# More slots of the expert loop per unit of work in nine stages of a two-layer kernel

## The reference

```python
def peer(h, w_q, keys, u, v):
    ...
    qh = (x @ w_q).reshape(T, PEER_HEADS, 2, PEER_HALF)
    s = jnp.einsum('thcd,hcnd->thcn', qh, keys).astype(jnp.float32)
    s1, i1 = lax.top_k(s[:, :, 0], PEER_TOPK)
    s2, i2 = lax.top_k(s[:, :, 1], PEER_TOPK)
    ...
    def block(args):
        xb, eb, gb = args
        act = jax.nn.gelu(jnp.einsum('thkd,td->thk', u[eb], xb))
        return jnp.einsum('thk,thkd->td', (gb * act).astype(xb.dtype), v[eb])
```

## Time and profile before

| | |
|---|---|
| time, median of 3 runs | 4246.91 us (4234.9 to 4251.95) |
| time of the profiled execution | 4234.23 us |
| its span, first to last instruction | 4232.1 us |
| busy share of the span | PE 70%, DVE 71%, POOL 38%, ACT 34% |
| DMA | 1521.91 MB, mean 360 GB/s |
| mean granted TensorE clock | 0.852 of 2.4 GHz |

### The profile page before, as it was taken

One profiled execution on the slowest core, in us unless ns is written; L12 is line 12 of the kernel. 1 busy time (PEld: TensorE's weight loads), 2 busy tenths in 40 slices (PEclk: granted clock), 3 DMA queues, 4 the chain that ended last, 5 costly groups with the idle time before them and its releaser, 6 DMA issues.

```text
span 4232.1 us, 32788 instructions
## 1 busy us (share of the span) xinstructions
PE 2981.6 (70%) x9343; PEld 1539.7 (36%) x9343; DVE 3022.8 (71%) x6125; ACT 1425.6 (34%) x4133; POOL 1623.8 (38%) x1311
## 2 busy tenths in 40 slices
PE   4699766876777645757778776868775887555565
PEld 1365352454433202423463233543453633212221
DVE  0406779978988666787669868769786787666666
ACT  1213323522233313246423333523552233322232
POOL 0001332434544434344334434435343345544554
PEclk8798887988989866878889988879887998897888
DMA  8243897989999997999899989999999999999998
GB/s 321 91 162 134 334 405 270 343 343 368 405 367 415 407 413 313 387 387 408 357 359 372 401 361 366 374 365 400 383 371 369 357 416 403 422 421 418 404 421 371
DMA packets 222323, 1521.91 MB, mean 360 GB/s; under 512 B 29758, under 2 KB 33538, under 8 KB 48823
## 3 DMA queue, kind: packets, MB, share of 16 engines
q0 software_dynamic: 187200, 1370.25, 80.6%
q1 hardware_dynamic: 34942, 149.58, 9.0%
HBM read 1516.49 MB, written 3.24 MB: 359 GB/s over the span
## 4 chain that ended last, share of the span: by engine, by line
DMA 31%; PE 30%; DVE 23%; issue 7%; ACT 4%; POOL 3%; DVEq 1%; SPq 1%; PEldq 1%; PEld 0%; ACTq 0%; POOLq 0%
DMA core_ring<-in_l_uv,core_experts 26%; PE sum_rows L1946 8%; DVE core_ring L1906 6%; DVE core_yv L1921 4%; POOL core_ring L1889 3%; PE sum_rows L2213 2%; PE j_in_ps L471 2%; PE j_query_pq L1679 1%; PE s1c_query_pq L1679 1%; PE s1b_in_ps L471 1%; DMA s0a_h_w<-in_l_peer_wq 1%; DMA mod_w<-in_l_w_mod 1%; DMA s1b_h_w<-in_l_peer_wq 1%; PE s0b_out_po L610 1%; DVEq L158 1%
## 5 line engine op out<-in xcount | busy, mean ns | idle before, releaser
L1889 POOL DMA_INDIRECT core_ring<-in_l_uv,core_experts x1280 | 1609.0, 1257 | 2259.7 <-PE sum_rows L1946 1081.4
L1946 PE MATMUL sum_rows<-core_ring,core_diag 128*128 128x512 f32 x3100 | 1681.3, 689 | 670.5 <-ACT core_diag L1935 540.3
L1906 DVE CUSTOM_DVE_ANT_0 core_ring<-core_ring,core_hc 128x1024 f32<-128x1024 f32 x1280 | 1551.8, 1223 | 723.6 <-DMA core_ring<-in_l_uv,core_experts 487.1
L1946 PEld LDWEIGHTS sum_rows<-core_ring,core_diag 128*128 128x128 f32 x3100 | 631.4, 217 | 1643.6 <-ACT core_diag L1935 897.0
L1929 ACT ACTIVATE core_wt<-core_wt 128x1 f32<-128x1 f32 x1280 | 256.5, 200 | 1675.0 <-DVE core_wt L1906 1583.3
L1921 DVE SCALAR_TENSOR_TENSOR core_yv<-core_ring,core_wt,core_yv 128x1024 f32<-128x1024 f32 x495 | 634.0, 1281 | 13.3 <-ACT core_wt L1932 12.8
L1932 ACT ACTIVATE core_wt<-core_wt,core_gates 128x1 f32<-128x1 f32 x1280 | 376.8, 294 | 41.6
L1935 ACT ACTIVATE core_diag<-core_ident,core_wt 128x128 f32<-128x128 f32 x775 | 311.2, 401 | 25.3
L2213 PE MATMUL sum_rows<-core_ring 128*128 128x416 f32 x320 | 118.4, 530 | 5.2 <-DVEq L158 4.1
L1929 ACT ACT_TABLE_LOAD x81 | 103.9, 1283 | 5.2 <-DVEq L158 3.8
L1906 DVE DVE_READ_ACCUMULATOR2_ANT core_wt<- 128x1 f32 x1280 | 104.9, 82 | 0.0
(11 more groups left out here) (772 smaller groups left out, 3055.7 us busy)
## 6 DMA issues: line engine op xcount, KB each, us to landing
mod_w<-in_l_w_mod SPq DMA_DIRECT2D x16, 2048.0 KB, 13.1
core_ring<-in_l_uv,core_experts POOLq DMA_INDIRECT x1280, 10.1
core_ring<-in_l_w_mod POOLq DMA_DIRECT2D x8, 2048.0 KB, 10.9
p_in_w<-in_l_w_in SPq DMA_DIRECT2D x5, 1664.0 KB, 8.9
core_ring<-in_l_w_in POOLq DMA_DIRECT2D x5, 1664.0 KB, 10.6
p_h_w<-in_l_peer_wq SPq DMA_DIRECT2D x16, 512.0 KB, 4.5
s0a_h_w<-in_l_peer_wq SPq DMA_DIRECT2D x16, 512.0 KB, 12.5
s0b_h_w<-in_l_peer_wq SPq DMA_DIRECT2D x16, 512.0 KB, 8.3
```

The lines of the kernel that those rows point to most:

```text
L1889: nc.gpsimd.indirect_dma_start(self.ring[:, r, :], None, core.a[f"l{layer}_uv"], bass.IndirectOffsetOnAxis(ap=self.experts[:, t, n:n + 1], ...
L1906: nc.vector.tensor_tensor_reduce(self.ring[:, r, 0:D], self.ring[:, r, 0:D], self.hc[:], 1.0, 0.0, ALU.mult, ALU.add, self.wt[:, r:r + 1]) ...
L1946: mm = nc.tensor.matmul(self.py[:, c * 512:(c + 1) * 512], self.diag[:, r, :], self.ring[:, r, D + c * 512:D + (c + 1) * 512], start=(at = ...
```

## The change

Nine stages get more slots per unit; leads and places stay.

```diff
-REST_RATES = {"norm": (3.0, PE_4, 5), "gla": (2.0, PE_6, 4), "pool": (2.0, PE_2, 4), "out": (1.5, PE_0, 3), "query": (2.0, PE_0, 2),
+REST_RATES = {"norm": (3.0, PE_4, 5), "gla": (2.0, PE_6, 4), "pool": (2.0, PE_2, 4), "out": (1.75, PE_0, 3), "query": (2.0, PE_0, 2),
...
-LATENT_RATES = {"norm": (3.0, PE_4, 5), "in": (1.0, PE_0, 4), "qk": (1.125, PE_4, 5), "attend": (2.25, PE_5, 3), "out": (1.6, PE_0, 3),
-                "query": (0.9, PE_0, 2), "first select": (2.0, PE_8, 3), "select": (2.1, PE_8, 3)}
+LATENT_RATES = {"norm": (3.0, PE_4, 5), "in": (1.4, PE_0, 4), "qk": (1.125, PE_4, 5), "attend": (2.25, PE_5, 3), "out": (1.9, PE_0, 3),
+                "query": (1.15, PE_0, 2), "first select": (2.0, PE_8, 3), "select": (2.1, PE_8, 3)}
...
-JOINT_RATES = {"norm": (3.0, PE_4, 5), "in": (1.4, PE_0, 4), "qk": (1.125, PE_4, 5), "attend": (2.25, PE_5, 3), "out": (1.6, PE_0, 3),
-               "query": (0.7, PE_0, 2), "first select": (2.0, PE_8, 3), "select": (2.1, PE_8, 3)}
+JOINT_RATES = {"norm": (3.0, PE_4, 5), "in": (1.7, PE_0, 4), "qk": (1.125, PE_4, 5), "attend": (2.25, PE_5, 3), "out": (2.0, PE_0, 3),
+               "query": (1.0, PE_0, 2), "first select": (2.0, PE_8, 3), "select": (2.1, PE_8, 3)}
```

## The result

The changed kernel takes 4191.64 us (median, 4186.9 to 4198.27), the kernel before, run beside it, 4249.43 us (4234.9 to 4260.77). By the medians that is 57.8 us less. The ratio of the runs is 0.9871, with a 95% interval of 0.985 to 0.9893, that is 45.5 to 63.7 us less. Forecast were 4207 us, 40 us less.

A forecast was written before the change was run, and what follows sets the result against it. Gathers bound the drain, while idle DMA time remained in the nine stages; -87.4 + 50.7 - 3 = -40 us took the profiled 4234.2 to 4194 us, or 4207 us against the sister runs' median, range 4172 to 4240.

The forecast's parts named there:

- 768's end: Slot 768's tile end leaves s1b query for the end of s1b out, where query chunks hide it: -6.5 us.
- 896's end: Slot 896's tile end leaves s1c out's first units for an attend stage: -3 + 1.6 us, bounds -6 and +2.
- 1024's end: Slot 1024's tile end moves into a select and stops the DMA there: +5.2 us, bounds 0 and +7.
- What it takes from the end: 34 slots leave the run to slot 384 (four) and the drain (thirty), 2.57 us each: 87.4 us less.
- What it adds to the stages: Nine stages take 34 more gathers, 87.4 us of DMA time, of which 36.7 us fill idle time: +50.7 us.
- The ends of tiles: The ends of slots 768, 896 and 1024 move to other stages: together about -3 us, from -12.5 to +9.
- The other start gaps: Idle DMA at the starts of four out stages, 24.9 us with s1c out's 7.4, was taken to stay unfilled.
- The full rate: 410 GB/s taken as full DMA rate in the nine stages, giving 72.2 us idle; at 425 GB/s, 93.3 us.
- the stages are full already: Rival: idle time in the nine stages may not be fillable; gain 0 to 21 us, 4226 to 4247 us; chance 0.20.
- the clock falls: Rival: PE's clock drops in j1 in, s1b in and two query stages; at 0.70, 4268 us; slower by over 0.5%: 0.05.
- The larger gain: Rival: full rate is 425 GB/s and out stages' start gaps shrink; 59 to 90 us less, 4157 to 4188; chance 0.09.

The follow-up runs named there:

- s0b out alone: Kernel before with only s0b out's rate raised, 1.5 to 1.75 (four slots): 4244.26 us, ratio 0.9999.
- The shift alone: Kernel before with layer 1's joint first select at 2.3 instead of 2.0, six slots more; the nine stages keep their slots: 4222.77 us, ratio 0.9949.
- the projections alone: Kernel before with only layer 1's two input projections raised, 1.4 to 1.7 and 1.0 to 1.4 (seven slots): 4213.87 us, ratio 0.9931.
- the queries alone: Kernel before with only layer 1's three query stages raised, 0.7 to 1.0 and 0.9 to 1.15 twice (thirteen slots): 4197.52 us, ratio 0.9889.
- the output stages alone: Kernel before with only layer 1's three output stages raised, 1.6 to 2.0 and 1.9 (ten slots): 4208.96 us, ratio 0.992.

## Why the prediction was right, and where its sum was off

The prediction's terms beside what the pair of profiles shows, in us. The ends' terms are put to their stages.

| | predicted | measured |
|---|---|---|
| drain, 30 slots | -77.1 | -75.2 |
| run to 384, 4 slots | -10.3 | -6.5 |
| s0b out | +4.4 | +9.6 |
| j1 in | +7.8 | +3.5 |
| j1 out | +10.2 | +6.4 |
| j1 query | +2.5 | +2.2 |
| s1b in | +3.9 | +3.9 |
| s1b out | +5.0 | +3.7 |
| s1b query (with 768's end, -6.5) | +3.7 | -1.4 |
| s1c out (with 896's end, -3) | +1.4 | -5.4 |
| s1c query | +2.3 | -0.7 |
| s1c attend (896's end) | +1.6 | +1.0 |
| last select (1024's end) | +5.2 | +6.2 |
| all other stages from s0b out on | 0 | +7.7 |
| sum (the prediction rounds to -40) | -39.4 | -45.0 |

**What it takes from the end** was right: the drain holds 225 slots in 580.7 us, 579 were forecast. The run to slot 384 gave 6.5 us instead of 10.3: thirteen slots took 36.4 us and nine take 29.86, so a slot less is not 2.57 us less there. The kernel with s0b out alone has the run at 29.4 us too.

**What it adds to the stages** was the step that was mis-sized. With the two ends that leave them the nine stages were to grow by 41.2 us, and grew by 21.8. Three of its parts were off that way:

- *The ends of tiles.* I took about -3 us for the three together. The shift alone, with no slot put into idle time, brings 9.6 us in s1b query and 9.1 in s1c out, for 2.6 and 4.0 paid in s1b out and the last select: -12 in the profile and -20.7 us (14 to 29) in the time. In the profile that is the lower bound which the prediction had given, -12.5; in the time it is beyond it. The step that failed is the one for slot 896: I said its end only coincided with the start gap of s1c out, which would stay. It was the gap: where 89 GB/s stood for 9.5 us, the kernel with the shift alone, at the stage's old rate, has 412 in the like place.

```profile
3223.70:3233.20 9.50, 6.07 (x22) 4.84 (x23) 9.16 (x12) 2.34 (x7) 5.07 (x5) 0.84 1.01 412
```

The kernels with the projections and with the queries alone have no such gap either. In the changed kernel the stage runs at 419 GB/s, and the 7.4 us that I had kept as not fillable are filled.
- *The other start gaps.* That of j1 out, 11 us at 67 GB/s, nearly closed as well. The 20 us from 20 us behind the stage's start, in the kernel before, with the projections alone (four slots shifted, old rate), with the output stages alone (new rate, nothing shifted) and in the changed kernel:

```profile
2101.80:2121.80 20.00, 14.89 (x58) 12.21 (x56) 10.86 (x15) 4.62 (x14) 4.29 (x3) 0.83 0.55 214
2116.40:2136.40 20.00, 15.89 (x62) 13.46 (x63) 12.54 (x17) 3.55 (x12) 5.92 (x4) 0.84 0.79 309
2112.30:2132.30 20.00, 14.94 (x58) 12.04 (x56) 12.10 (x16) 4.18 (x15) 6.61 (x6) 0.83 0.69 274
2119.80:2139.80 20.00, 14.32 (x56) 12.17 (x56) 13.82 (x18) 3.77 (x17) 6.92 (x5) 0.84 0.92 375
```

The shift alone closes a part of it. The rate alone comes near the spread, for the five kernels that have neither are at 193 to 251 GB/s. At the new rate two slots follow the first unit instead of one, with the same lead. I had written that j1 out is the exception there, and then left its 9.2 us out with the rest. The gap of s1b out did stay (205 GB/s from 2800 to 2808 us in the changed kernel), and the stage grew nearly as forecast.

- *The full rate.* I took the drain's 410 GB/s as full in all stages. Where weights and gathers run side by side it is higher: j1 in ran at 421 over its whole length, s1b query at 417, s1c out at 419, while the drain stayed at 408. That is about half of why j1 in grew by 3.5 us and not by 7.8: by rate and length it moved 34.2 MB for 30.8, which at 410 GB/s would have made it 5.7 us longer; four whole gathers would be 4.2 MB. The Trainium skill puts the ceiling of the fabric that the DMA engines share at 435 GB/s ("DMA: Bandwidth & Descriptors", Specifications), from which I had estimated 68 us to be fillable as against 36.7. No stage of any run here came to that: the fastest, j1 in of the kernel with the projections alone, had 424.

**Off in the other direction** was s0b out. Its four slots cost 9.6 us there and bring 10.3 at most; alone they bring nothing (0.9999). I had let 5.9 us of idle time be filled, since DVE was busy for only 85.9 of 113.8 us. A mean over the stage hid that DVE is full in the last norm units, where the DMA has room; I had seen that in j1 out's tail and counted it there alone. With half of the adds on PE that stretch did fill, and the stage hardly got shorter, so this is a part of the cause, and the rest stays open.

**Not in the sum** were the stages whose slots keep their number. Together they took 7.7 us more in this pair. Two of the larger differences are no effect of the change. The joint norm, 2.9 us longer, is as long in the kernels with the projections alone, with the output stages alone and with the shift, which are the kernel before up to there. Layer 1's modulation, 3.6 us shorter, is short in this one profile alone. Three return in the other kernels with the same slots: the second of s0b's selects (+4.0 here, 2.1 to 4.5 in all five with the new rate in s0b out), j1's second select (+3.0, and 1.8 to 3.0 in the five kernels that hold the same slots there) and s1b qk (+3.4, and 1.2 to 3.4 in the same five). In the two selects the gap at a tile's end got longer; the end stands four and fourteen slots earlier in the stage's own order. The 15 us of the gap in the second of s0b's selects, before:

```profile
1247.00:1262.00 15.00, 7.79 (x12) 3.34 (x13) 14.72 (x57) 4.99 (x17) 4.94 (x4) 0.58 0.35 113
```

In the changed kernel the DMA nearly stops for the 15 us:

```profile
1258.00:1273.00 15.00, 6.65 (x9) 2.86 (x10) 14.69 (x51) 3.38 (x12) 2.29 (x2) 0.52 0.07 19
```

DVE is full in both. In the changed kernel sixteen steps of the select's top 16 stand ahead of the tile's last dot product, and only at 1262.56 us comes the first of the end's three sums; before, eight shorter steps stood there. I priced one such end, that of 1024, at 5.2 us (6.2 measured), and not the change in those of 256 and 640.

**The rivals.** That the stages are full already falls by the rates, 410 to 421 GB/s where it was 341 to 397. For s0b out its price came true. That the clock falls did not happen: j1 in has 0.94, j1 query 0.96, s1b in 0.92, s1c query 0.97, where 0.93, 0.95, 0.91 and 0.95 stood. The larger gain, 59 to 90 us, was the nearest of the three by its conditions: a full rate above 410 and gaps that close, and both came true in part. The 57.8 us lie just below it. What it lacked is that a gap can be an end of a tile.

What the pair of profiles leaves open is the rest between its 45.0 us and the 57.8 of the medians. Single profiles spread that much: in the kernels with s0b out alone and with six slots more in a full stage (0.9999 and 0.9998) the stretch from s0b out on is 9.1 us longer and 7.9 us shorter than before. So the rows of the table, each from one pair, are sure to a few us only, and that the rest is spread is likely and not shown.

## What to carry to other kernels

When background work is shifted in a static order, first list the points where it must stop (here the end of each tile) and see beside what each falls after the shift: the same stop cost some 7 us of DMA time or nothing, and what told the two apart was whether another queue still had bytes to move. Idle time is worth filling only where no engine of the chain is full in that same stretch, so read windows of 10 to 20 us, not a stage's mean. Parts that each win alone do not add up when they share such a shift; one kernel that only shifts, in a stage that is full, shows how much is shared.

## What the runs showed of the hardware

The gathers alone hold 408 to 411 GB/s, at a DMA share of 0.99, in every drain of these runs. With SP's weight chunks beside them the same 16 engines move more over whole stages, at a share of 1.01 to 1.02: j1 in with 24 slots 421 to 424 GB/s in six of the seven kernels that have it (411 in the one with more slots in the norms), s1b query with 20 slots 417 to 419. I had not expected that the mixture is the faster one by 2 to 3 per cent, for 1.05 MB gathers in rows of 8 KB. And 411 GB/s held for 9 us in which POOL issued one gather, at 2846.8 us, since the weight queue carried half of it and gathers issued earlier the other half.
